# A one-core model block: the first norm rewritten, and the first chunks of the conv output projection reordered

## The reference, cut to what matters

```python
def rms_norm(x, g):
    xf = x.astype(jnp.float32)
    y = xf * lax.rsqrt(jnp.mean(xf * xf, axis=-1, keepdims=True) + EPS)
    return (y * g.astype(jnp.float32)).astype(x.dtype)

def conformer_conv(h, w_in, dw, dw_b, ln_g, ln_b, w_out):
    u = h @ w_in
    a, b, z = jnp.split(u, 3, axis=-1)
    v = a * jax.nn.sigmoid(b)
    ...                                     # 31 taps along the tokens, per channel
    v = jax.nn.silu(layer_norm(v, ln_g, ln_b))
    return (v * jax.nn.silu(z)) @ w_out
...
h = rms_norm(x, conv_norm[j]);  x = x + conformer_conv(h, ...)
```

## Time and profile before

| what | value |
|---|---|
| median of 3 runs | 2482.45 us (2481.13 to 2483.45) |
| the profiled execution | 2483.07 us, of which the span is 2481.3 us |
| PE busy | 2355.5 us, 95% of the span |
| DVE, ACT, POOL busy | 1575.3, 1269.2, 226.5 us |
| mean granted TensorE clock | 0.973 of full |
| moved by transfers | 409.47 MB, 165 GB/s |

### The profile page before, as it was taken

The page is one execution under the profiler, slowest core; times in us unless marked ns, Lnnn a source line. Parts: engine busy times, 40 slices in busy tenths (PEclk is TensorE's granted clock), DMA queues, the critical chain, the costliest instruction groups (busy, mean ns, idle before and its releaser), DMA issues.

```text
span 2481.3 us, 37445 instructions
## 1 busy us (share of the span) xinstructions
PE 2355.5 (95%) x14320; PEld 2084.3 (84%) x14320; DVE 1575.3 (63%) x2308; ACT 1269.2 (51%) x1375; POOL 226.5 (9%) x53
## 2 busy tenths in 40 slices
PE   7999988999999999989899987977999999999999
PEld 6999977888888888878788866866888888888888
DVE  4777766667666666666566655664565555555566
ACT  5556554566666566445566665444433334433333
POOL 3777720000000000000000000000000000000000
PEclk9999989899999999999999989998999999999999
DMA  5444435344444443536344421541455555555556
GB/s 219 168 172 171 170 141 190 146 169 154 165 158 153 154 154 135 180 143 230 144 152 153 152 85 68 189 150 68 159 190 191 188 187 186 187 188 191 184 199 220
DMA packets 57283, 409.47 MB, mean 165 GB/s; under 512 B 6352, under 2 KB 6480, under 8 KB 8400
## 3 DMA queue, kind: packets, MB, share of 16 engines
q1 hardware_dynamic: 57168, 407.82, 45.7%
HBM read 405.70 MB, written 2.10 MB: 164 GB/s over the span
## 4 chain that ended last, share of the span: by engine, by line
PE 85%; DVE 5%; ACT 5%; issue 3%; DMA 2%; DVEq 0%; SPq 0%; ACTq 0%
PE G L346 22%; PE G L345 22%; PE G L344 11%; PE G L347 11%; PE G L353 3%; PE G L354 3%; PE G L355 3%; DMA RAW<-stream_dram 2%; ACT HI L322 1%; PE A L903 1%; DVE LO L329 1%; PE A L890 1%; PE A L930 1%; DVE HN L449 1%; DVE A L728 0%
## 5 line engine op out<-in xcount | busy, mean ns | idle before, releaser
L322 ACT ACTIVATE HI<-RAW 128x2048 fp32r<-128x2048 f32 x381 | 728.0, 1913 | 847.5 <-DMA RAW<-stream_dram 847.2
L329 DVE TENSOR_TENSOR LO<-RAW,HI 128x2048 fp32r<-128x2048 f32 x332 | 760.4, 2291 | 378.9 <-ACT HI L322 376.8
L346 PE MATMUL G<-HX,HI 128*128 128x512 f32 x2056 | 835.3, 406 | 45.7 <-DVE HX L468 21.4
L345 PE MATMUL G<-HX,HI 128*128 128x512 f32 x2056 | 820.5, 399 | 0.0
L344 PE MATMUL G<-HX,LO 128*128 128x256 f32 x2056 | 577.2, 281 | 0.0
L347 PE MATMUL G<-HX,LO 128*128 128x256 f32 x2056 | 575.9, 280 | 0.0
L344 PEld LDWEIGHTS G<-HX,LO 128*128 128x128 f32 x2056 | 391.3, 190 | 95.6
L347 PEld LDWEIGHTS G<-HX,LO 128*128 128x128 f32 x2056 | 392.5, 191 | 86.8
L346 PEld LDWEIGHTS G<-HX,HI 128*128 128x128 f32 x2056 | 395.9, 193 | 53.6 <-DVE HX L468 22.9
L345 PEld LDWEIGHTS G<-HX,HI 128*128 128x128 f32 x2056 | 390.2, 190 | 0.0
L336 POOL TENSOR_TENSOR LO<-RAW,HI 128x2048 fp32r<-128x2048 f32 x49 | 226.3, 4618 | 104.0 <-ACT HI L322 103.3
(11 more groups left out here) (339 smaller groups left out, 2568.5 us busy)
## 6 DMA issues: line engine op xcount, KB each, us to landing
RAW<-stream_dram SPq DMA_DIRECT2D x381, 1024.0 KB, 4.8
X<-x_dram SPq DMA_DIRECT2D x4, 512.0 KB, 5.1
MB<-mem_dram SPq DMA_DIRECT2D x4, 512.0 KB, 5.6
out_dram<-X SPq DMA_DIRECT2D x4, 512.0 KB, 7.7
CON<-constants_dram SPq DMA_DIRECT2D x1, 981.0 KB, 16.2
VEC<-vectors_dram SPq DMA_DIRECT2D x1, 623.5 KB, 17.2
VEC<-vectors_dram SPq DMA_DIRECT2D x1, 280.0 KB, 6.5
CON<-constants_dram SPq DMA_DIRECT2D x1, 64.5 KB, 1.8
```

The source lines that it names most:

```text
L322: nc.scalar.activation(HI[:, c.slot(RING), :], RAW[:, c.slot(RING), :], ACT.Copy).then_inc(hi_ready, 1)
L329: nc.vector.tensor_tensor(LO[:, c.slot(RING), :], RAW[:, c.slot(RING), :], HI[:, c.slot(RING), :].bitcast(F32), ALU.subtract).then_inc(lo_ ...
L345: return nc.tensor.matmul(res, wh, both[:, k, :, :], start=False, stop=last)
L346: nc.tensor.matmul(res, wh, both[:, k, :, :], start=first, stop=False)
```

## The change

At the start, the 16 norm weights get a transfer of their own ahead of X. ScalarE loads the table for Ln at once, squares into `SZ` (16 tiles wide, so no buffer is waited for), and also multiplies the weights into tiles 8 to 15. VectorE adds the squared tiles together, so that TensorE has one matmul with ones left; it multiplies the weights into tiles 0 to 7 ahead of `RR`, and afterwards only `RR` itself, in wide instructions over `CV`. The fill of `HX` is cut finer (`START`: 2, 2, 4, 4, 4 tiles), and `gemm_two` gets a `lag`: chunk 1 runs two groups behind chunk 0. In `conv_out` ScalarE's `split_hi` of chunk 49 goes ahead of the first `high`, and VectorE's adds of each chunk go ahead of its `split_lo`.

```diff
-FILLS = [EVEN, TWOS, EVEN, EVEN, EVEN, EVEN, EVEN, EVEN, EVEN[:1], EVEN]
+START = [(0, 2), (2, 4), (4, 8), (8, 12), (12, 16)]
+FILLS = [START, TWOS, EVEN, EVEN, EVEN, EVEN, EVEN, EVEN, EVEN[:1], EVEN]
...
-        def gemm_two(pe, c, r, h, paired=True, operand=None):
+        def gemm_two(pe, c, r, h, paired=True, operand=None, lag=0):
...
-            for g, (k0, k1) in enumerate(FILL[h]):
-                pe.wait_ge(h_ready, h + g + 1)
-                for m in range(2):
+            groups = FILL[h]
+            for step in range(len(groups) + lag):
+                for m, g in ((0, step), (1, step - lag)):
+                    if not 0 <= g < len(groups):
+                        continue
+                    if m == 0 or not lag:
+                        pe.wait_ge(h_ready, h + g + 1)
...
+        def start_act(act, n):
+
+            act.preload_act_table_set("natural_log")
             for g in range(KT // GRP):
-                act.wait_ge(s_x[g], 16 if g else 32)
-                wait(act, n_ss, n.sq(GRP * (g - 1)))
-                nc.scalar.activation(HN[:, g % 2], X[:, g * GRP:(g + 1) * GRP, :], ACT.Square).then_inc(n_sq, GRP)
...
+                act.wait_ge(s_x[g], 16 if g else 48)
+                nc.scalar.activation(SZ[:, g * GRP:(g + 1) * GRP, :], X[:, g * GRP:(g + 1) * GRP, :], ACT.Square).then_inc(n_sq, GRP)
...
+            gained(8, 12)
+            split_hi(act, At(0))
+            n.root(act)
+            high(0)
+            split_hi(act, At(1))
+            high(1)
+            gained(12, 16)
+            for g in range(2, len(START)):
+                high(g)
+            act.wait_ge(s_vec, 16)
+
+        def start_pe(pe, n):
+            pe.wait_ge(s_x[0], 48)
+            pe.wait_ge(n_ss, START_ADDS)
+            nc.tensor.matmul(A[n.bank][:, 0:T], ONES, LR[:], start=True, stop=True).then_inc(n_ss, KT - START_ADDS)
...
+            scaled(0)
+            scaled(1)
+            low(0)
+            scaled(2)
+            low(1)
+            split_lo(dve, At(1))
+            scaled(3)
+            low(2)
+            scaled(4)
+            low(3)
+            low(4)
...
-                        if first and j == 0 and self.ahead > 2:
-                            wait(dve, lo_ready, c + self.ahead)
-                        if not (last and j + self.ahead > 5):
-                            split_lo(dve, c + self.ahead)
+                        if self.ahead == 2:
+                            split_lo(dve, c + 2)
...
+                        if self.ahead > 2 and not (last and j + self.ahead > 5):
+                            if first and j == 0:
+                                wait(dve, lo_ready, c + self.ahead)
+                            split_lo(dve, c + self.ahead)
...
-                if g == 1:
+                if g == 0:
                     split_hi(act, At(C_CONVO + 1))
...
             sp.dma_start(CON[:, 0:K_FIRST], constants[:, 0:K_FIRST]).then_inc(s_x[0], 16)
+            sp.dma_start(VEC[:, 0:KT], vectors[:, 0:KT]).then_inc(s_x[0], 16)
             for g in range(0, KT, GRP):
                 sp.dma_start(X[:, g:g + GRP, :], x_in[:, g:g + GRP, :]).then_inc(s_x[g // GRP], 16)
-            sp.dma_start(VEC[:, 0:V_FIRST], vectors[:, 0:V_FIRST]).then_inc(s_vec, 16)
+            sp.dma_start(VEC[:, KT:V_FIRST], vectors[:, KT:V_FIRST]).then_inc(s_vec, 16)
```

More of the change, by code:

```diff
@@ L385, in gemm_two @@
                         wait(pe, g_free[(r + m).slot(NG)], (r + m).turn(NG))
-                    for k in range(k0, k1):
+                    for k in range(*groups[g]):
                         if paired:
@@ L390, in gemm_two @@
                             mm = product3(gres(r + m), c + m, k, both, k, k == 0, k == KT - 1)
-                    if k1 == KT:
+                    if g == len(groups) - 1:
                         mm.then_inc(mm_done, 1)
@@ new lines, in gained, with high @@
+            def gained(k0, k1):
+                for ft in range(k0, k1):
+                    ins = nc.scalar.activation(CV[:, ft, :], X[:, ft, :], ACT.Copy, scale=vec(n.gain, ft))
+                ins.then_inc(n_zero, 1)
+            def high(g):
+                k0, k1 = START[g]
+                act.wait_ge(n_hn, g + 1)
+                nc.scalar.activation(HH[:, k0:k1, :], CV[:, k0:k1, :], ACT.Copy).then_inc(n_hh, 1)
+            gained(8, 12)
+            split_hi(act, At(0))
+            n.root(act)
@@ new lines, in start_act, with start_dve, gained, scaled @@
+            high(0)
[9 more added lines that the diff above has]
+            nc.tensor.matmul(A[n.bank][:, 0:T], ONES, LR[:], start=True, stop=True).then_inc(n_ss, KT - START_ADDS)
+        def start_dve(dve, n):
+            def gained(k0, k1):
+                for ft in range(k0, k1):
+                    ins = nc.vector.tensor_scalar(CV[:, ft, :], X[:, ft, :], vec(n.gain, ft), None, ALU.mult)
+                return ins
+            dve.wait_ge(s_x[0], 48)
+            gained(0, 4)
+            for g in range(1, KT // GRP):
+                dve.wait_ge(n_sq, GRP * (g + 1))
+                wait(dve, n_ss, g - 1)
+                nc.vector.tensor_tensor(SZ[:, 0:4, :], SZ[:, 0:4, :], SZ[:, 4 * g:4 * g + 4, :], ALU.add).then_inc(n_ss, 1)
+            dve.wait_ge(n_ss, 3)
+            nc.vector.tensor_tensor(SZ[:, 0:2, :], SZ[:, 0:2, :], SZ[:, 2:4, :], ALU.add).then_inc(n_ss, 1)
+            dve.wait_ge(n_ss, 4)
+            nc.vector.tensor_tensor(LR[:], SZ[:, 0, :], SZ[:, 1, :], ALU.add).then_inc(n_ss, 1)
+            dve.wait_ge(s_x[1], 16)
+            gained(4, 8).then_inc(n_zero, 1)
+            split_lo(dve, At(0))
+            dve.wait_ge(n_rr, 1)
+            def scaled(g):
+                k0, k1 = START[g]
+                dve.wait_ge(n_zero, 1 + (k0 >= 8) + (k0 >= 12))
+                nc.vector.tensor_tensor(CV[:, k0:k1, :], CV[:, k0:k1, :], RR[:].unsqueeze(1).broadcast_to([P, k1 - k0, T]),
+                                        ALU.mult).then_inc(n_hn, 1)
+            def low(g):
+                k0, k1 = START[g]
+                dve.wait_ge(n_hh, g + 1)
+                nc.vector.tensor_tensor(HL[:, k0:k1, :], CV[:, k0:k1, :], HH[:, k0:k1, :].bitcast(F32), ALU.subtract).then_inc(h_ready, 1)
+            scaled(0)
[9 more added lines that the diff above has]
+            low(4)
+            dve.wait_ge(s_vec, 16)
@@ L2275, in _ @@
         def _(act):
[L2276 to L2279 removed]
+            start_act(act, norm_conv)
             split_hi(act, At(2))
```

20 lines of the change are left out of this document (6 added, 14 removed).

## The result

| | before | after |
|---|---|---|
| median of 5 runs each, same chip | 2482.45 us (2478.16 to 2486.86) | 2468.62 us (2463.18 to 2471.53) |
| ratio of the two, 95% interval | | 0.9941 (0.9929 to 0.9954) |
| the profiled execution, and its span | 2483.07, 2481.3 | 2469.33, 2467.6 |
| mean granted TensorE clock | 0.973 | 0.977 |

The account below looks back on a forecast made before the run. TensorE, busy 95% of the span, was taken to bound the kernel, with time to be had only where it idles or runs at the lower clock. 3.6+0.5+6.1 = 10.2 us gave 2472.3 us, range 2468.5 to 2477.5.

Parts of the forecast that it names:

- the three terms: Gains at the start (3.6 us), ahead of conv_out (0.5) and in conv_out (6.1); all within about 1.5 us: chance 0.62.
- low end: Whole kernel: bottom of the range, 2468.5 us, from a best case of 2470.0 less 1.3 of run spread.
- the sum itself: Whole kernel: gains at the start, ahead of conv_out and in it add to 10.2 us, giving 2472.3.
- simply move forward by the sum: Stages behind the touched code: shift earlier by the 10.2 us total; otherwise the prediction is wrong.
- the sum's first term: Start: earlier products and no wait ahead of chunk 5, which begins at 55.4 instead of 58.95; gain 3.6 us.
- The small transfer: Start: norm weights' transfer ahead of X costs 0.45 us, bounds nothing and 1.8; rival of held X alone, chance 0.06.
- Terms 2 and 3: Ahead of conv_out, earlier rounding of chunk 49, 0.5 us; in conv_out, stop ahead of chunk 51 and lower clock gone, 6.1.
- The stop did not move: conv_out rival: late split of chunk 52 moves the stop ahead of it, 2476.0; chance 0.10 shared with clock staying low.
- the short stop ahead of chunk 50: conv_out rival: this 0.36 us stop keeps the lower clock, losing 2.7, 2475.0; chance 0.10 shared with the stop moving.
- The rival on the slow side: conv_out: late squares' add delays splits, each of 15 chunks stops, 2487; slower or no visible change, chance 0.03.

Follow-up runs that it names:

- one_vec: The changed kernel with the vectors in one transfer, whole and ahead of X, instead of two; 2466.61 us, ratio 0.9927 to the kernel before.
- hi49_only: The kernel before with only ScalarE's rounding of chunk 49 moved ahead of the first rounding of the gated tiles; 2480.87 us, ratio 0.9995.
- start_only: The changed kernel with both edits ahead of and in conv_out taken back, leaving the new start; 2471.41 us, ratio 0.9958 to the kernel before.
- no_lag: The changed kernel without lag=2 in the first pair of chunks; 2469.85 us, ratio 0.9949 to the kernel before.
- early_gates: The changed kernel with ScalarE's gates of chunks 46 and 47 moved to earlier rounds; 2458.10 us, ratio 0.9907 to the kernel before.
- pe_pad: The changed kernel with 15 matmuls without use put back on TensorE at the start; 2471.11 us, ratio 0.9944 to the kernel before.
- group2_first: The changed kernel with HX's third group ahead of chunk 1's split (VectorE) and the weights of tiles 12 to 15 (ScalarE); 2468.20 us, ratio 0.9942.
- before_again: The kernel before, unaltered, profiled once more for a second trace; 2486.18 us in a single run.

## Why the prediction was right or wrong

The direction and the mechanisms of the three terms held. But the time is 3.7 us below the forecast by the median (2468.62, which by 0.1 us still lies in the range) and 4.5 by the ratio (2467.8, which lies below its low end of 2468.5). That low end is itself set 0.2 us lower than its own working, 2470.0-1.3 = 2468.7.

*The step that failed most is the sum itself,* "3.6+0.5+6.1 = 10.2 us": it has no term for anything behind `conv_out`, because I held that the later stages "simply move forward by the sum". They did not. The stage from chunk 63 to 73, in code that nobody touched, takes 75.3 us on the mean of the change's three traces and 79.2 on the seven with the old start, 3.9 us less; in the pair of traces that I predicted from it is 4.1. There the touched places brought less than forecast (3.0 and 6.2), so the whole excess over 10.2 is this stage and small differences elsewhere. Its price is the stop in the first head (2.17 against 3.78 us) and the lower clock behind it, and the stop follows the landing of chunk 69.

*The second step is the sum's first term,* "Gain: 58.95-55.4 = **3.6 us**", which was too small by 1.2. The laying out of the new order held to 0.7 us: first product 18.7 (19.38), steady from 25.75 (26.17), the feed's end 29.4 (29.6), no wait ahead of chunk 5. What it was set against was not typical. I took the start of before, with its first product at 23.93, from one execution, and that was a good one: over the seven traces of the old start chunk 5 ends at 65.5 to 69.4, mean 67.0; over the three of the change at 61.7 to 62.8, mean 62.2. The term is 4.8 on the mean and anything from 2.7 to 7.7 in a pair. The earlier trace rows held the hint: ScalarE's last square waited for TensorE's sums, which ran at whatever clock was granted. I wrote that the new order needs no buffer, but priced it with the one waiting time seen. In the pair that I predicted from, the term came out at 3.0, because of two small errors: chunk 0 was rounded at 13.10 rather than 12.55, and the lower clock lasted 5.3 us of steady work instead of 4.5 (3.3 and 4.1 in the change's two other traces).

*The small transfer* cost about twice what I took, but within its bounds: the first square began at 5.32, the last X landed at 9.79 and chunk 0 at 13.07, 0.9 and 1.0 us later than in the trace of before, where I had put 0.45 (0.7 and 0.7 against the means of the seven traces). The Trainium skill (DMA: Bandwidth & Descriptors, Anatomy of one DMA) gives the 2.0 us of fixed cost as a fit for transfers that GpSimd issues, and puts most of it down to the completion; these are SP's. It did not show in full as a delay of what stands behind it, and `one_vec`, where all the vectors go ahead of X, begins at 5.64 and ends chunk 5 at 62.2.

*Terms 2 and 3* were right in size. From the end of chunk 47 to that of 52 the three traces of the change take 36.9 us on the mean, those with the old `conv_out` order 43.5 (six of them, `hi49_only` apart): 6.6, against 0.5+6.1. The stop did not move, and the short stop ahead of chunk 50 did not bring the lower clock. The rival on the slow side found nothing: no splitting in `conv_out` came late.

*The account* on the means, 4.8+6.6+3.9 = 15.3, compares with a measured 13.8 to 14.6. It agrees within the spread of single executions, no closer: behind chunk 73, where no version differs, the 19 traces take 1969.9 to 1975.7 us, and the change's own three differ there by 4.2.

*Open.* Why `start_only` gains 7 us or more by its ratio, where its trace shows some 4 at the start, is not explained, and so the change's time may hold a gain that no stage here shows. With the new start the code packet comes at the end of chunk 69's transfer or behind it, and yet it landed after 7.4 us in `start_only`, 7.1 in `no_lag` and 7.5 in `early_gates`, with stops of 3.51, 3.23 and 3.51; so other things move it as well. A code packet is also neither needed nor enough: over the 19 traces, of the weight transfers (from the ninth on) with one in their first 4 us, 18 to 27 in a trace, 153 of 403 landed after more than 5.8 us, median 5.48; of all others 164 of 6684, median 4.78. What makes just these late is not settled, nor why `early_gates` had no lower clock behind its 3.51 us.

## What to carry to other kernels

Read the stage that you mean to change in several executions before you price it: where one engine waits for another whose speed depends on the granted clock, a single trace can be off by as much as the change brings. When a wait has gone, look at the next one ahead of it: here two gates moved forward on ScalarE brought as much again (7.3 us in their stage) as the whole planned edit ahead of and in `conv_out` (6.6). A stage without slack can change by microseconds when a transfer that it waits for lands sooner or later, and that moved here with the length of TensorE's code, so an edit is not priced by its own place alone.

## What the runs showed of the hardware

- A stop of TensorE costs in two steps. In the first head, stops of 3.13 us and more in the traces with the old start, in `no_lag` and in `pe_pad` were followed by the lower clock (0.50 for 3 to 5.5 us), those of 1.4 to 2.8 us in the change, `one_vec` and `group2_first` were not; but one of 3.51 us was followed by it in `start_only` and not in `early_gates`, and ahead of chunk 5 stops of 1.85 and 1.87 us were followed by it (`hi49_only`, `before_again`), those of 1.29 to 1.79 not.
- Sixteen sums on an otherwise idle TensorE took 8.84 or 10.20 us in the same kernel, by the moment at which the higher clock was granted.
- Code transfers of 16 KB run beside the weights; three watched chunks landed later in the traces where one fell well inside their own transfer: 69 after 7.3 to 8.6 us against 5.7 to 7.5, 228 after 5.8 to 6.3 against 4.7 to 4.9, 231 after 5.8 to 6.5 against 4.7 to 5.0.
- Executions of one kernel spread over up to 9 us, roughly in step with the granted clock: the five of the change took 2463.18 at 0.979 and 2471.53 at 0.976.
